# Gate-and-up products of three feed-forward layers, split into two products on the row halves of the array and added by VectorE

## The reference, cut to what matters

```
def swiglu_ffn(x, w_gate, w_up, w_down):
    return (jax.nn.silu(x @ w_gate) * (x @ w_up)) @ w_down
```

## Time and profile before

| | |
|---|---|
| median of three runs | 3001.75 us |
| runs | 3004.93, 3001.75, 2999.98 us |
| span of the profiled execution | 3001.9 us |
| TensorE busy | 95% of the span |
| VectorE, ScalarE, GpSimd busy | 35%, 33%, 40% |
| granted TensorE clock, mean | 0.970 |

### The profile page before, as it was taken

One profiled execution on the slowest core, in us unless ns is written; L12 is line 12 of the kernel. 1 busy time (PEld: TensorE's weight loads), 2 busy tenths in 40 slices (PEclk: granted clock), 3 DMA queues, 4 the chain that ended last, 5 costly groups with the idle time before them and its releaser, 6 DMA issues. The chain is left out here.

```text
span 3001.9 us, 35277 instructions
## 1 busy us (share of the span) xinstructions
PE 2837.8 (95%) x14172; PEld 2240.4 (75%) x14172; DVE 1050.6 (35%) x1692; ACT 996.8 (33%) x1422; POOL 1197.6 (40%) x414
## 2 busy tenths in 40 slices
PE   8999999999889998989999999889999989999998
PEld 7887878788679788768887688356786636788876
DVE  2110123989343562241110300566404345611103
ACT  3221232233544514342221332245224445422212
POOL 4443553455455237344444442111342221544443
PEclk9999999999999999999999999989999989999999
DMA  4222232234300153112222133110331101222221
GB/s 161 98 98 97 86 112 81 87 126 147 120 1 1 36 198 119 57 70 98 98 98 90 65 126 149 57 73 15 134 112 71 60 35 56 71 98 98 98 87 68
DMA packets 42118, 266.51 MB, mean 89 GB/s; under 512 B 4240, under 2 KB 5648, under 8 KB 13968
## 3 DMA queue, kind: packets, MB, share of 16 engines
q1 hardware_dynamic: 38400, 256.47, 23.4%
q10 hardware_dynamic: 3600, 8.39, 0.7%
HBM read 248.07 MB, written 16.78 MB: 88 GB/s over the span
## 5 line engine op out<-in xcount | busy, mean ns | idle before, releaser
L214 POOL TENSOR_TENSOR weights_lo<-weights_raw,weights_hi 128x2048 fp32r<-128x2048 f32 x193 | 900.7, 4667 | 1462.3 <-ACT weights_hi L203 1462.2
L244 PE MATMUL psum<-x_hi,weights_hi 128*128 128x512 f32 x2274 | 901.2, 396 | 8.2 <-POOL weights_lo L214 3.3
L245 PE MATMUL psum<-x_lo,weights_hi 128*128 128x512 f32 x2274 | 891.1, 392 | 0.0
L246 PE MATMUL psum<-x_hi,weights_lo 128*128 128x512 f32 x2274 | 890.6, 392 | 0.0
L203 ACT ACTIVATE weights_hi<-weights_raw 128x2048 fp32r<-128x2048 f32 x193 | 369.5, 1915 | 768.8 <-PE psum L246 730.9
L244 PEld LDWEIGHTS psum<-x_hi,weights_hi 128*128 128x128 f32 x2274 | 431.4, 190 | 120.2 <-issue 26.0
L246 PEld LDWEIGHTS psum<-x_hi,weights_lo 128*128 128x128 f32 x2274 | 430.6, 189 | 91.3
L245 PEld LDWEIGHTS psum<-x_lo,weights_hi 128*128 128x128 f32 x2274 | 431.4, 190 | 89.0 <-issue 0.7
L467 DVE SCALAR_TENSOR_TENSOR arena<-arena,psum 128x512 f32<-128x512 f32 x66 | 45.4, 687 | 566.7 <-PE psum L246 558.9
L244 PE MATMUL psum<-h_hi,weights_hi 128*128 (+1 forms) x528 | 208.2, 394 | 7.3 <-PEq L424 7.3
L246 PE MATMUL psum<-h_hi,weights_lo 128*128 (+1 forms) x528 | 206.7, 391 | 0.0
(11 more groups left out here) (398 smaller groups left out, 3513.4 us busy)
## 6 DMA issues: line engine op xcount, KB each, us to landing
weights_raw<-in_stream SPq DMA_DIRECT2D x201, 1024.0 KB, 4.8
keep_gates<-arena ACTq DMA_DIRECT2D x24, 256.0 KB, 2.0
arena<-keep_gates SPq DMA_DIRECT2D x3, 2048.0 KB, 9.5
arena<-keep_x SPq DMA_DIRECT2D x3, 2048.0 KB, 7.9
keep_x<-arena SPq DMA_DIRECT2D x2, 2048.0 KB, 9.3
arena<-in_w_k SPq DMA_DIRECT2D x2, 2048.0 KB, 9.1
arena<-in_na_bias SPq DMA_DIRECT2D x1, 3584.0 KB, 11.4
keep_x<-arena ACTq DMA_DIRECT2D x1, 2048.0 KB, 6.7
```

The costliest lines, as they stand in the source:

```text
L214: K.nc.gpsimd.tensor_tensor(K.wlo[:, 1 - slot, :, :], K.raw[:, 1 - slot, :, :], K.whi[:, 1 - slot, :, :].bitcast(F32), ALU.subtract).then_ ...
L244: K.nc.tensor.matmul(out, whi, xhi, start=start, stop=False)
L245: K.nc.tensor.matmul(out, whi, xlo, start=False, stop=False)
L246: return K.nc.tensor.matmul(out, wlo, xhi, start=False, stop=stop)
```

## The change

Every matmul of these phases but those of ffn1_in's first tile becomes two: one over rows 0 to 63 of the contraction, one over rows 64 to 127, each into a bank of its own. The lower half goes into the bank as before, the upper half into one of banks 4 to 7. VectorE copies the upper bank to SBUF (into the place that SiLU or the product will overwrite), and adds it to the lower bank in PSUM; ScalarE's SiLU waits for the gate's sum, and VectorE's product for up's. The special first chunk of ffn2_in and ffn3_in is gone: all six products of a chunk (twelve halves) now wait for `x_split`.

```
+UPPER = {0: (5, 6), 1: (4, 7)}
+ROWS = (slice(0, P // 2), slice(P // 2, P))
+
+def three_products_by_rows(K, lower, upper, whi, wlo, xhi, xlo, start, stop):
+    for w, x, first, last in ((whi, xhi, start, False), (whi, xlo, False, False), (wlo, xhi, False, stop)):
+        for out, rows in ((lower, ROWS[0]), (upper, ROWS[1])):
+            ins = K.nc.tensor.matmul(out, w[rows], x[rows], start=first, stop=last)
+    return ins
+
+def pair_pe(K, pe, name, t0=0, split=False, turned=0):
...
+    def body(t, g, uses, slot, times):
+        pe.wait_ge(K.s("lo_ready").sem, g + 1)
+        for j in range(2):
+            pe.wait_ge(free[j].sem, free[j].at(t + (t0 - 1)))
+            for k in range(KC):
+                last = half(slot, j, k)
+            last.then_inc(done[j].sem, 1)
+
+    if split:
...
+        for k in range(KC):
+            pe.wait_ge(K.s("x_split").sem, K.s("x_split").at(k + 1))
+            for j in range(2):
+                last = half(slot, j, k)
+                if k == KC - 1:
+                    last.then_inc(done[j].sem, 1)
+    tile_loop(pe, name, body, peeled=1)
...
-                stream_pe(K, pe, name, peeled=1)
+                pair_pe(K, pe, name, turned=turned)
             else:
-                stream_pe(K, pe, name, split=norm is not None)
+                pair_pe(K, pe, name, split=True, turned=turned)
...
-                wait_bank(K, act, g, 0)
+                act.wait_ge(gate_sum.sem, gate_sum.at(t + 1))
                 nc.scalar.activation(sg[:, slot, :], K.ps[:, 2 * slot, :], ACT.Silu).then_inc(silu.sem, silu.n(1, times))
...
+                wait_bank(K, dve, g, 0)
+                if whole:
+                    nc.vector.nop().then_inc(gate_sum.sem, gate_sum.n(1, times))
+                else:
+                    nc.vector.tensor_copy(sg[:, slot, :], gate_upper).then_inc(gate_moved.sem, gate_moved.n(1, times))
+                    dve.wait_ge(gate_moved.sem, gate_moved.at(t + (0 if first_tile else 1)))
+                    nc.vector.tensor_tensor(gate, gate, sg[:, slot, :], ALU.add).then_inc(gate_sum.sem, gate_sum.n(1, times))
                 wait_bank(K, dve, g, 1)
+                if not whole:
+                    nc.vector.tensor_copy(h[:, slot, :], up_upper).then_inc(up_moved.sem, up_moved.n(1, times))
+                    dve.wait_ge(up_moved.sem, up_moved.at(t + (0 if first_tile else 1)))
+                    nc.vector.tensor_tensor(up, up, h[:, slot, :], ALU.add).then_inc(up_sum.sem, up_sum.n(1, times))
+                    dve.wait_ge(up_sum.sem, up_sum.at(t + (0 if first_tile else 1)))
                 dve.wait_ge(silu.sem, silu.at(t + 1))
```

More of the change, by code:

```diff
@@ L246, in three_products, with half @@
     return K.nc.tensor.matmul(out, wlo, xhi, start=False, stop=stop)
+UPPER = {0: (5, 6), 1: (4, 7)}
[6 more added lines that the diff above has]
+def pair_pe(K, pe, name, t0=0, split=False, turned=0):
+    free = [K.s("bank_free_0"), K.s("bank_free_1")]
+    done = [K.s("first_done"), K.s("tile_done")]
+    def half(slot, j, k):
+        return three_products_by_rows(K, K.ps[:, 2 * slot + j, :], K.ps[:, UPPER[slot ^ turned][j], :], K.whi[:, slot, 8 * j + k, :],
+                                      K.wlo[:, slot, 8 * j + k, :], K.xhi[:, k, :], K.xlo[:, k, :], k == 0, k == KC - 1)
+    def body(t, g, uses, slot, times):
[6 more added lines that the diff above has]
+    if split:
+        g = span(name)[0]
+        slot = g % 2
+        pe.wait_ge(K.s("lo_ready").sem, g + 1)
+        for j in range(2):
+            pe.wait_ge(free[j].sem, free[j].at(t0 - 1))
+        for k in range(KC):
+            pe.wait_ge(K.s("x_split").sem, K.s("x_split").at(k + 1))
+            for j in range(2):
+                last = half(slot, j, k)
+                if k == KC - 1:
+                    last.then_inc(done[j].sem, 1)
+    tile_loop(pe, name, body, peeled=1)
 def stream_pe(K, pe, name, n=T, t0=0, split=False, x=None, ready="x_split", mid=None, peeled=0):
@@ L423, in phase_ffn_in @@
     sg, h = K.A[:, 52:54, :], K.A[:, 54:56, :]
+    turned = FIRST_TILE[name] % 2
+    first_tile = isinstance(norm, FirstSplit)
+    gate_sum, gate_moved, up_moved, up_sum = K.s("gate_sum"), K.s("gate_moved"), K.s("up_moved"), K.s("up_sum")
     with nc.Block() as block:
@@ L464, in evac @@
             def evac(t, g, slot, times):
-                wait_bank(K, dve, g, 1)
+                whole = first_tile and isinstance(t, int) and t == 0
+                gate, up = (K.ps[:, 2 * slot + j, :] for j in range(2))
+                gate_upper, up_upper = (K.ps[:, UPPER[slot ^ turned][j], :] for j in range(2))
+                wait_bank(K, dve, g, 0)
[5 more added lines that the diff above has]
+                    nc.vector.tensor_tensor(gate, gate, sg[:, slot, :], ALU.add).then_inc(gate_sum.sem, gate_sum.n(1, times))
+                wait_bank(K, dve, g, 1)
+                if not whole:
[3 more added lines that the diff above has]
+                    dve.wait_ge(up_sum.sem, up_sum.at(t + (0 if first_tile else 1)))
                 dve.wait_ge(silu.sem, silu.at(t + 1))
-                nc.vector.scalar_tensor_tensor(h[:, slot, :], sg[:, slot, :], weight, K.ps[:, 2 * slot + 1, :],
+                nc.vector.scalar_tensor_tensor(h[:, slot, :], sg[:, slot, :], weight, up,
                                                ALU.mult, ALU.mult).then_inc(h_ready.sem, h_ready.n(1, times))
@@ L476, in evac @@
                                         ALU.subtract)
-            stream_dve(K, dve, name, evac)
+            evac(0, FIRST_TILE[name], FIRST_TILE[name] % 2, 1)
+            tile_loop(dve, name, lambda t, g, uses, slot, times: evac(t, g, slot, times), peeled=1)
     K.end_block()
```

## The result

| | before | after |
|---|---|---|
| median | 3001.75 us | 3010.98 us |
| lowest to highest of 5 runs | 2999.49 to 3004.93 | 3008.64 to 3012.82 |
| ratio, 95% interval | | 1.0027 [1.0014, 1.0039] |
| span of the profiled execution | 3001.9 us | 3010.9 us |

The change makes the kernel slower by 9.2 us between the medians (0.31%); the ratio over all runs says 0.27%. The forecast was 9.75 us on the same median (3011.5). The profiled executions differ by 9.0 us.

The account below looks back on a forecast made before the run. The prediction took the changed phases as bound by TensorE, number of matmuls by pace. With pace unchanged, 5.6 + 1 + 3 = 9.6 us on 3001.9 gave 3011.5 us; the range for 8 in 10 was 2972 to 3055.

Parts of the forecast that it names:

- The pace of a pair: Gate-and-up matmuls: two half products take one whole product's 226.7 ns, no change; chance 0.58.
- faster: Rival for the pairs: the 13.4 ns beyond a matmul's columns are hidden, -42 us at full price, 2970 us; chance 0.17.
- each half pays: Rival for the pairs: the stops of both halves add up, 240 ns a pair, +42 us, 3053 us; chance 0.12.
- one after the other: Rival for the pairs: the halves run serially, 453 ns a pair, +707 us, 3719 us; chance 0.10.
- Loop turns: Rival in TensorE's loops: doubled instructions make it fetch its program again, 27 turns at 2 us, +54 us; chance 0.03.
- The three ends: Ends of the three phases: an uncovered copy and sum before VectorE's product, 1.86 us three times, +5.6 us.
- My lower bound of 1.38 us: Each phase end: copy and sum if the waits for VectorE's own results cost nothing, +4.1 us in all.
- The clock behind them: Behind the phase ends: longer idle likely drops the third end's clock as well, +1 us; bounds 0 and +4.
- The starts of ffn2_in and ffn3_in: First chunk: all six pairs wait for `x_lo`, 1.5 us each, +3 us.
- the clock also rises later: Starts of ffn2_in and ffn3_in: the matmuls that raise the clock start 2.06 us later, costing at most 1 us.
- VectorE within a tile: Inside each tile: 2.8 us of added copies and sums fit, SiLU comes 1.9 us later, TensorE doesn't wait.
- Smaller things: Switches between whole and half rows at phase edges: a few tenths of a us in all, counted at nothing.

Follow-up runs that it names:

- The lower halves alone: Changed kernel without the upper half products and without VectorE's copies and sums: 3429.47 us; with whole first tiles in ffn2_in and ffn3_in too, 3008.89 us.
- the blocks of 3, 6, 12 and 24: Changed kernel with lower halves grouped ahead of upper: 3 and 3, 3016.12 us; 6, 12 and 24 in ffn1_in, ffn2_in and ffn3_in, 3284.25 us.
- The sums alone: Kernel before, whole products, with VectorE given a copy of each bank and a maximum with that copy: 3013.31 us, ratio 1.0029.
- the last tile whole: Changed kernel with whole products in the last tile of each of the three phases: 3007.37 us, ratio 1.0018.
- the first chunk: Changed kernel with the first chunk's `x_hi` pairs in ffn2_in and ffn3_in waiting for `x_hi_done` alone: 3011.99 us, ratio 1.0027.
- both together: Changed kernel with whole last tiles and the first chunk's early products given back as pairs: 3006.15 us, ratio 1.0009; run again, 3005.74 us, ratio 1.0017.

## Why the prediction was right

**The pace of a pair: right.** 226.7 ns measured, 226.7 forecast, in ffn1_in and, once warm, in the other two. The 213.3, 240 and 453 ns of the bounds are excluded, and with them the rivals "faster", "each half pays" and "one after the other". The lower halves alone also take 226.7 ns each, so the 13.4 ns belong to a load and a matmul on the same rows, and the other half's work neither hides them nor adds to them. The Trainium skill ("TensorE: Matmul & The Clock Gate", Part 3) has matmuls start strictly in the program's order; the blocks of 3, 6, 12 and 24 show otherwise for halves on different rows, by three or four places. What happens inside the array during those 13.4 ns no run shows.

**Loop turns: right.** Turns of 192 matmuls and as many weight loads show no gap: 228.29 busy of 228.30 us. No run shows the 2 us that this rival took for a turn.

**The three ends: right in kind, forecast 5.6 us, measured 4.4.** Each gap grew by 1.46 us. The mis-sized part is the wait for VectorE's own result: 0.24 us was taken from the product-to-cast wait of the earlier trace rows, which is still 0.25 us. But copy, sum and product now start at 252.63, 253.35 and 254.09, 0.72 and 0.74 us apart for 0.69 us of work: 0.04 us each. My lower bound of 1.38 us lay nearer. "The sums alone" (4.28 us) and "the last tile whole" (2.82 us) show that the growth comes from the copy and the sum.

**The clock behind them: forecast 1 us, 3.8 by the table.** (2.14 - 0.88) x 3; in the two profiles of this comparison alone it is 6.1 less 3.3, 2.8 us. I had counted the third end alone, two times in three. All three lose, the second for longer. The 3.8 lie inside the bound of 4.

**The starts of ffn2_in and ffn3_in: forecast 3 us, measured 1.6.** The two phases, counted as above, are 0.80 and 0.82 us longer in the profile, and "the first chunk" takes 0.64 and 0.79 of that back. The first matmul is indeed 2.1 us later (6.05 against 3.92 us of idle), and the end of the first chunk some 1.4 us. What failed is the step "the clock also rises later". It rises later by the first matmul, but no later by the work: 11 matmuls ran at the slow level before, in 6.13 us with two waits for `x_lo` among them, and 11 pairs do now, in 4.72 us without a wait. That gives back the waits that the second chunk had before.

**VectorE within a tile: "it fits, no wait" right, its working wrong.** I moved SiLU by 1.9 us, to 107.9, and it came at 109.46. The step that failed is the cast taken at 0.43 us wherever it stands. Moved beside GpSimd's subtraction it takes 4.47, and all of VectorE's later work is queued behind it. VectorE is busy 173.5 us of the stretch instead of some 97, and the 4 us of cover I named are 1.13 us. By an estimate from that row, ScalarE's rounding would have been late had GpSimd's work been 1.2 us longer. That was not among my rivals.

**Smaller things: counted at nothing, measured 0.25 us.** That is the one switch from whole to half rows that stands inside a stream, in ffn1_in ("both together" above).

**The sum.** 4.4 + 3.8 + 1.6 + 0.25 = 10.1 us, measured 9.2. The forecast's 5.6 + 1 + 3 is 9.6, from three terms that are each wrong in size and cancel. The agreement to 0.5 us is luck; what held was that pace costs nothing, and that ends, starts and clock together cost under 0.5%. Nor is the sum as closed as it looks. The kernel of "both together", whose ends and starts are those of before, still lies 3 to 6 us above it, and "the last tile whole" lies 5.6 us above it where the starts (1.6) and four switches (1.0) are explained. If that surplus is in the changed kernel too, the sizes above leave no room for it. Stretches that no variant touches differ by up to 5 us between executions (1075.6 to 1081.0 us for the one between ffn1_in and ffn2_in). In the two profiles compared here the terms come to 4.4 + 2.8 + 1.6 + 0.25 = 9.1 of 9.0 us only because such differences cancel: apart from the clock behind the ends, the changed kernel's profile is 0.5 us shorter in ffn1_in's first tile and ahead of it, 2.8 us shorter between ffn1_in and ffn2_in, and 3.3 us longer between ffn2_in and ffn3_in, 2.8 of them behind the wait at 2521.14.

## What to carry to other kernels

Splitting a full contraction of 128 rows into halves doubles the instructions and buys no time, since the pair moves at one product's pace; what it costs is what must put the halves together where nothing covers it: the last tile of a phase, and the idle time of TensorE there, which also costs its clock.

When work is put on an engine, look not only at whether it fits but at where it pushes the operations behind it: here a cast of 0.43 us came to stand beside GpSimd's subtraction and took 4.5 us, and 1.1 us of reserve was left.

A forecast that comes out to 0.5 us is no proof of its terms; the gaps, the starts and the clock read one by one put them off by a quarter, by nearly double and by a factor of 3.8.

## What the runs showed that I had not expected

- A half product runs ahead of three or four halves for the other rows that stand before it: blocks of 6 and 6 bring a tile from 10.88 to 11.00 us, 12 and 12 to 15.7 us, 24 and 24 to 18.8 us.
- Halves over 64 rows alone leave the clock at 0.50 for the whole of two phases (420 us lost), and keep it at 1.00 behind one tile of whole products.
- Gaps of the same length in the same program differ in what the clock does behind them: 0.12 or 1.7 us lost behind 2.8 us. One wait of 2.57 us, the same in every profile, costs 2.8 us in four of them.
- A VectorE operation with one operand in PSUM runs at its usual length beside GpSimd's subtraction (0.69 us), where those with all operands in SBUF take some 4 us longer.
